# A chunked RWKV-7 scan on one core: state products taken by tokens, another order of the pass, the block solver shared between two engines

## The reference, cut to what matters

```python
def _rwkv_step(S, inp):
    r, w, kk, kka, kt, v = inp
    sk = jnp.einsum('bhij,bhj->bhi', S, kk)
    S = S * w[:, :, None, :] - sk[..., None] * kka[:, :, None, :] + v[..., None] * kt[:, :, None, :]
    return S, jnp.einsum('bhij,bhj->bhi', S, r)
```

## Time and profile before

| | us |
|---|---|
| median of 3 runs (3841.2 to 3844.97) | 3842.14 |
| profiled execution | 3850.02 |
| its span | 3848.3 |
| TensorE busy in the span | 3417.3 (89%) |
| VectorE, ScalarE, GpSimd busy | 1747.0, 1178.4, 552.4 |

### The profile page before, as it was taken

One profiled execution on the slowest core, in us unless ns is written; L12 is line 12 of the kernel. 1 busy time (PEld: TensorE's weight loads), 2 busy tenths in 40 slices (PEclk: granted clock), 3 DMA queues, 4 the chain that ended last, 5 costly groups with the idle time before them and its releaser, 6 DMA issues.

```text
span 3848.3 us, 65362 instructions
## 1 busy us (share of the span) xinstructions
PE 3417.3 (89%) x28861; PEld 2311.7 (60%) x28861; DVE 1747.0 (45%) x2909; ACT 1178.4 (31%) x2057; POOL 552.4 (14%) x754
## 2 busy tenths in 40 slices
PE   6999989999999898745776899898989999989998
PEld 5777776343343766545664443236757888756887
DVE  4324641121222654963356222126855546855454
ACT  3225722111111565921112111003253234334233
POOL 2220120000000210048513000001102210101210
PEclk8999998999999998867888899999999999989999
DMA  6531147989886352987533999993203313212322
GB/s 246 184 107 52 61 167 266 375 313 370 317 313 262 124 182 98 313 223 183 145 102 133 344 415 420 419 420 133 88 22 118 113 62 107 70 54 99 101 86 77
DMA packets 314859, 739.32 MB, mean 192 GB/s; under 512 B 68248, under 2 KB 148896, under 8 KB 265424
## 3 DMA queue, kind: packets, MB, share of 16 engines
q1 hardware_dynamic: 302480, 697.18, 49.7%
q0 software_dynamic: 12096, 37.96, 3.1%
HBM read 673.19 MB, written 61.89 MB: 191 GB/s over the span
## 4 chain that ended last, share of the span: by engine, by line
PE 70%; DVE 10%; DMA 8%; ACT 5%; issue 2%; SPq 2%; POOL 0%; DVEq 0%; POOLq 0%; ACTq 0%
PE ps L62 66%; DMA raw<-in_moe_w_dram 6%; PE ps L66 4%; SPq L120 2%; DVE mx L75 1%; DVE mx L102 1%; DVE mrn L99 1%; DVE b L75 1%; DVE cr L75 1%; DMA Tb<-ot 1%; DVE o L75 1%; DVE o L81 0%; ACT cr L72 0%; DMA c<-in_w_ple_gate_dram 0%; ACT lw L72 0%
## 5 line engine op out<-in xcount | busy, mean ns | idle before, releaser
L62 PE MATMUL ps<-raw,xinT 128*64 128x512 f32 (+1 forms) x4096 | 591.6, 492 | 32.8 <-DMA raw<-in_moe_w_dram 23.6
L62 PEld LDWEIGHTS ps<-raw,xinT 128*64 128x64 f32 (+1 forms) x4096 | 196.0, 123 | 401.4 <-issue 288.1
L62 PE MATMUL ps<-wp,hp 128*128 128x512 f32 x1024 | 314.1, 393 | 8.6 <-ACT wp L72 8.6
L62 PE MATMUL ps<-cr,oTr 128*128 128x512 f32 (+2 forms) x1024 | 255.6, 382 | 3.5 <-ACT oTr L72 3.1
L75 DVE TENSOR_TENSOR mx<-mx,ps 128x512 f32<-128x512 f32 (+1 forms) x196 | 127.3, 663 | 234.6 <-PE ps L62 133.3
L62 PEld LDWEIGHTS ps<-wp,hp 128*128 128x128 f32 x1024 | 193.8, 190 | 49.0 <-issue 8.8
L62 PEld LDWEIGHTS ps<-cr,oTr 128*128 128x128 f32 x1024 | 187.6, 188 | 38.9 <-ACT oTr L72 3.6
L62 PE MATMUL ps<-wp,hTr 128*128 128x512 f32 x512 | 194.4, 389 | 0.0
L62 PE MATMUL ps<-raw,hidT 128*64 128x512 f32 x768 | 177.9, 602 | 3.2 <-DMA raw<-in_moe_w_dram 3.2
L62 PE MATMUL ps<-ar,naxh 128*128 128x512 f32 x576 | 147.4, 406 | 19.0 <-DVE ar L75 8.8
L75 DVE TENSOR_TENSOR wp<-c,wp 128x1536 fp32r<-128x1536 f32 x32 | 60.6, 1894 | 180.7 <-ACT wp L72 180.7
(11 more groups left out here) (535 smaller groups left out, 6332.4 us busy)
## 6 DMA issues: line engine op xcount, KB each, us to landing
raw<-in_moe_w_dram SPq DMA_DIRECT2D x384, 1024.0 KB, 7.7
c<-in_w_in_dram SPq DMA_DIRECT2D x28, 2048.0 KB, 9.3
mx<-in_ada_w_dram SPq DMA_DIRECT2D x14, 2048.0 KB, 8.0
raw<-in_ada_w_dram SPq DMA_DIRECT2D x8, 2048.0 KB, 13.5
a<-in_na_w_qkv_dram SPq DMA_DIRECT2D x6, 2048.0 KB, 7.9
c<-in_w_branch_dram SPq DMA_DIRECT2D x16, 512.0 KB, 5.9
c<-in_w_out_dram SPq DMA_DIRECT2D x4, 2048.0 KB, 10.8
c<-in_w_ple_gate_dram SPq DMA_DIRECT2D x4, 2048.0 KB, 7.9
```

Of the source, the lines that this page charges most:

```text
L62: return self.e.matmul(out, lhsT, rhs, start=start, stop=stop, skip_group_check=True) if self.e is not None else self
```

## The change

- A by features, R, B and K are laid out as [R0, A0, A1, R1] and [B0, K0, K1, B1] (0 and 1 the halves of 64 tokens), so that a Gram product takes 128 columns of B and K against 128 of A and R: half as many products of twice the size. R and B are loaded in halves of 64 tokens.
- X and Y are one product: for a latent pass the output has 128 partitions, half of them X's tokens and half Y's. `y1` and `y2` go. What `y3` did comes as `y`, added into X's banks, and is done one half later, alternating with the products of `u` (`products_u`, `products_y`); X's banks are held until then. Y now lies by tokens, is copied by ScalarE (added by VectorE from step 4 on), and the readout needs no turn through TensorE.
- `v` and `s` are one product over 128 rows: V and U lie in one tile `VU` (two buffers), V loaded per pass and half, and the token rows of B and K in the matching halves. One bank instead of two; VectorE's sum is one operation, its decay two.
- Transfers: `load` 8 or 12, `load_m` 12, `load_t` 4. V for the readout (4 chunks) is loaded at pass 2.
- The solver: VectorE does chunk 0, rows 1 to 10 of chunk 1, and rows 24 to 31 of every later chunk as well, these at the head of an odd pass; GpSimd the rows between. The triangles of chunks 1 and 2 are loaded right behind chunk 0's. `store(n)` is in the list, at the head of the odd pass before it is used.
- `emm`: two additions instead of 22. Some tiles move into others that are free. `Banks.take` gives the free bank that was last used or released longest ago.

The diff, cut to its core (signs as in the diff; a few plain lines keep their place):

```diff
@@ class Banks @@
-        b = self.next % 8
-        self.next += 1
+        b = next(x for x in self.queue if x not in self.held.values())
+        self.last(b)
...
     def release(self, key):
-        del self.held[key]
+        self.last(self.held.pop(key))
@@ def rw_scan_order @@
     const()
-    load(0)
-    load_m(0)
-    load(1)
-    load_m(1)
+    for r in range(2):
+        load(r)
+        load_m(r)
+    rows(0, 1, 31)
+    store(0)
+    load_t(0)
     for s in range(4):
         gram(0, s)
     recur(0, 0, 'x1')
-    some(1)
-    load_t(0)
+    for n in range(1, 6):
+        rows(n, 1, LATE - 1)
     blocks(0)
     level(0, 0)
     level(0, 1)
     for r in range(12):
-        more = r + 1 < 12
+        more, n = r + 1 < 12, (r + 1) // 2
+        whole = more and r % 2
+        if more and not whole:
+            load_t(r + 1)
+        if more and r:
+            load_m(r + 1)
         if r + 2 < 12:
             load(r + 2)
-        if more:
+        if whole:
+            rows(n, LATE, 31)
+            store(n)
             load_t(r + 1)
-        some(3 if r else 8)
         recur(r, 0, 'x2')
-        recur(r, 0, 'y1')
-        recur(r, 0, 'y2')
-        one(r)
-        recur(r, 0, 'u')
-        recur(r, 0, 'v')
         if more:
             gram(r + 1, 0)
-            gram(r + 1, 1)
...
+        recur(r, 0, 'u')
+        one(r)
+        recur(r, 1, 'x1')
         recur(r, 0, 's')
         one(r)
+        if more:
+            gram(r + 1, 1)
+        one(r)
+        recur(r, 1, 'x2')
         if more:
             gram(r + 1, 2)
+            blocks(r + 1)
+        one(r)
+        recur(r, 1, 'u')
+        if more:
             gram(r + 1, 3)
+        recur(r, 1, 's')
         one(r)
...
         if more:
             level(r + 1, 0)
+            recur(r + 1, 0, 'x1')
             level(r + 1, 1)
         if r in (2, 9):
             rows_in(r)
+    recur(12, 0, 'u')
@@ def rw_scan, TensorE @@
+                for c in range(2):
+                    cols = pair(c) if lat(r) else keys(c)
+                    for p in range(2):
+                        k = 2 * g + i
+                        ins = e.matmul(P.psum[:, banks[p], i * 256 + cols.start:i * 256 + cols.stop], bk(r, z)[half(p), k, pair(c)], ar(r, z)[half(p), k, cols],
+                                       (i, c) == (0, 0), True)
...
+        def products_u(r, i, h):
+            b = P.banks.place.get(('u', r, i), 0)
+            for z in range(2):
+                o = half(1 - cut(z, i))
+                yield e.matmul(P.psum[o, b, sh(h)], Z(r, z)[o, h, :], X[o, sh(h)], h == 0, True)
+
+        def products_y(r, i, k, turn):
+            for z in range(2):
+                c, p = cut(z, i), z ^ turn
+                h = 2 * k + p
+                yield e.matmul(P.psum[half(c), P.banks.place.get(('x', r, i, p), 0), bank_of(z, k)], G(r, z)[half(1 - c), h, reads(c)],
+                               VU(r, z)[half(1 - c), i, sh(h)], False, True)
...
+                            out = P.psum[:, banks[p], bank_of(z, k)] if lat(r) else P.psum[half(1 - c), banks[p], bank_of(z, k)]
+                            ins = e.matmul(out, G(r, z)[half(c), h, pair(c) if lat(r) else keys(c)], VU(r, z)[half(c), i, sh(h)],
+                                           k == 0 and (turn == 0 or not lat(r)), False)
...
+                            ins = e.matmul(P.psum[half(p), b, bank_of(z, k)], tm(r, z)[:, c, sh(h)], VU(r, z)[:, i, sh(h)], (z, k) == (0, 0), True)
@@ def rw_scan, VectorE @@
+        def solve(n, i):
+            if n == 0 or i >= LATE or (n == 1 and i <= FIRST):
+                if n and i == LATE:
+                    e.wait_ge(*P.pool.at('row', n, i - 1))
+                solve_row(e, P.dve, n, i)
...
+            if what == 'u':
+                q, j = late(r, i)
+                if q >= 0 and step(q) >= 4:
+                    e.wait_ge(*P.pe.at('y', q, j))
+                    for z in range(2):
+                        for yo, src in parts(q, j, z):
                             e.tensor_tensor(yo, yo, src, ADD).then_inc(*P.dve.inc())
@@ def rw_scan, SyncE @@
+            squares(e, 0)
             fence(P, e, 'rw_features', *stored)
+            for n in (1, 2):
+                squares(e, n)
...
+        def store(n):
+            e.wait_ge(*P.dve.at('row', n, 31))
             for z in range(2):
+                e.dma_start(Td[z][ORDER[z][n]].rearrange("h (d n) -> (h d) n", d=4), Tv_of(n)[64 * z:64 * z + 64]).then_inc(*s_td[n].inc())
+            s_td[n].name('td', n)
+            if 1 <= n < 4:
+                squares(e, n + 2)
...
+                e.dma_start(ar(r, z)[:, :, 64:192], src['a']).then_inc(*s_ar[r % 3].inc())
+                e.dma_start(bk(r, z)[:, :, 64:192], src['k']).then_inc(*s_bk[r % 2].inc())
+                for c in range(2):
+                    if lat(r):
+                        e.dma_start(ar(r, z)[:, :, reads(c)], src['r'][:, :, half(c)]).then_inc(*s_ar[r % 3].inc())
+                    e.dma_start(bk(r, z)[:, :, reads(c)], src['b'][:, :, half(c)]).then_inc(*s_bk[r % 2].inc())
...
-                e.wait_ge(*P.pe.at('s', r - 2, 1))
+                e.wait_ge(*P.pe.at('recur', r - 2))
             for z in range(2):
...
+                for c in range(2):
+                    t = slice(chunk(r, z) * 128 + 64 * c, chunk(r, z) * 128 + 64 * c + 64)
+                    e.dma_start(VU(r, z)[half(c), cut(z, c), :], vd[t, f]).then_inc(*s_vu[r % 2].inc())
+                    e.dma_start(tm(r, z)[half(c), c, :], Tm['b', z][t, f]).then_inc(*s_tm[r % 2].inc())
+                    e.dma_start(tm(r, z)[half(1 - c), c, :], Tm['k', z][t, f]).then_inc(*s_tm[r % 2].inc())
```

More of the change, by code:

```diff
@@ L2757, in rows, with rw_scan_order @@
         self.s_g.name('readout')
-def rw_scan_order(const, load, load_m, load_t, gram, blocks, level, recur, solve, read, rows_in):
-    rows = iter(range(187))
+def rw_scan_order(const, load, load_m, load_t, gram, blocks, level, recur, solve, store, read, rows_in):
     reads = iter(READ)
-    def some(k):
-        for u in itertools.islice(rows, k):
-            solve(u)
     def one(r):
@@ L2773, in one, with rows @@
                 read(*x)
-    some(31)
+    def rows(n, first, last):
+        for i in range(first, last + 1):
+            solve(n, i)
     const()
-    load(0)
-    load_m(0)
-    load(1)
-    load_m(1)
+    for r in range(2):
[4 more added lines that the diff above has]
+    load_t(0)
     for s in range(4):
@@ L2971, in recur @@
                 for p in range(2):
-                    b, free = P.banks.take(('x', r, i, p), (P.act, 'x', r, i), hold=True)
+                    b, free = P.banks.take(('x', r, i, p), (P.dve if step(r) >= 4 else P.act, 'y' if lat(r) else 'x', r, i), hold=True)
                     banks.append(b)
@@ L3026, in recur @@
+                if q >= 0:
+                    for p in range(2):
+                        P.banks.release(('x', q, j, p))
+                    if j:
+                        P.pe.name('recur', q)
+            if what == 's' and not last:
+                e.wait_ge(*s_tm[r % 2].at('tm', r))
+                b, free = P.banks.take(('s', r, i), (P.dve, 'sum', r, i))
                 for f in free:
                     e.wait_ge(*f)
-                for h in range(8):
-                    for z in range(2):
-                        c = half(cut(z, i))
-                        ins = e.matmul(P.psum[c, b, sh(h)], Z(r, z)[c, h, :], XU[c, 0, sh(h)], h == 0, True)
@@ L3032, in recur @@
-                ins.then_inc(*P.pe.inc('u', r, i))
-            if what == 'v' and not last:
-                e.wait_ge(*s_tm[r % 2].at('tm', r))
-                banks = []
-                for z in range(2):
-                    b, free = P.banks.take(('s', r, i, z), (P.dve, 'sum', r, i, z), hold=True)
-                    banks.append(b)
-                    for f in free:
-                        e.wait_ge(*f)
-                for k in range(4):
-                    for z in range(2):
-                        for p in range(2):
-                            c, h = half(cut(z, i)), 2 * k + p
-                            ins = e.matmul(P.psum[half(p), banks[z], sh(k)], tm(r, z)[c, 0, sh(h)], V[c, chunk(r, z), hd(r, h)], k == 0, False)
-                ins.then_inc(*P.pe.inc())
@@ L3278, in load_t @@
         def load_t(r):
-            for z in range(2):
-                e.wait_ge(*s_td[z].at('td', step(r)))
+            e.wait_ge(*s_td[step(r)].at('td', step(r)))
             if r:
```

377 lines of the change are left out of this document (154 added, 223 removed).

## The result

The changed kernel takes 3946.51 us in the median (3946.09 to 3953.47, four runs), against 3843.55 for the kernel before on the same chip: 1.0273 times as long, with a 95% interval of 1.0255 to 1.0290. It is slower, as forecast, but by 103 us and not by 16; the range (up to 3882) does not hold it.

What follows compares the result with a forecast made beforehand. The scan was taken as a chain with no engine full. Start +2, leg 0 -1.1, legs 1 to 9 +19.3, leg 10 -4.0 and the rest 0 gave +16 us, 3866 profiled, so 3858 us in the median; range 3815 to 3882.

Steps and rivals of the forecast that it cites:

- the issue term of SyncE's chain: Odd legs of the scan: SyncE issues 24 token and feature transfers before the store, 12.3 us, taken as 13.5.
- the rule of banks: All stages: taking the oldest free bank adds no nameable TensorE wait elsewhere; 0, and -3 to +3 us if mergers reorder.
- TensorE's products: Latent scan passes: 768 matmul instructions fall to 512, some 2.6 us a leg by array time; typical even leg 21.2 us.
- The odd legs: Scan: late y, SyncE's loads, store, T's block load, VectorE and TensorE follow in a chain, 37.2 us a leg.
- Nothing hides it: Odd legs: no TensorE or VectorE work can cover the chain of 37.2 us, since all stands behind it in their queues.
- idle prices: Rival, odd legs: SyncE's chain holds but transfers land as in an empty queue, 30.5 us a leg, 3825 us; chance 0.24.
- TensorE alone bounds: Rival, scan: T is ready when wanted, so odd legs equal even ones at 21 us each, 3778 us; chance 0.08.
- 256-byte packets: Scan loads of R and B in halves: a 256-byte packet costs near 19 ns, making the loads 9.0 us of transfer.
- The rival of 32 ns: Rival, scan loads: 256-byte packets cost 32 ns, odd latent legs grow by 3.3 us, 3879 us; chance 0.16.
- r = 11 and the turns 0: Scan's end: one more y and its copy, +3 us, against two turns through TensorE lost, -3; together 0.
- Issue falls to 2 to 3 us a leg: Sign, scan: TensorE's waits for its own instructions, 4.1 us a leg before, fall to 2 to 3 us.
- Start "+2": Ahead of the scan's first product: solver rows moved to VectorE and 40 SyncE transfers before the first store, 2 us later.

Runs made afterwards that it cites:

- e3: The changed kernel with the store and the load of T's blocks ahead of the 24 token and feature loads in odd passes: 3893.29 us, ratio 1.0106.
- e9: The changed kernel with load(r+2) ahead of load_m(r+1), waiting for its buffer's last reader instead of the late Y: 3909.69 us, ratio 1.0166.
- e6: The changed kernel with x1 and x2 on 64x64 tiles and T's stores, block loads and later squares issued by GpSimd: 3873.54 us, ratio 1.0062.
- e7: As e6, but with the old rule of banks (next free one in a round) from the second network on: 3849.53 us, ratio 1.0000.
- e4: The changed kernel with each latent product x1 and x2 as two on 64x64 tiles, the same sums: 3920.69 us, ratio 1.0181.

## Why the prediction was right in sign and wrong in size

Three terms of the sum failed: the price of `x1` and `x2` on wide tiles, the issue term of SyncE's chain, and the rule of banks, which stood at nothing. The alternation of the legs and the chain of the odd ones were as forecast, though TensorE's wait in leg 5 was 16.9 us for 10 to 14 and the store started 22.3 us after S(5) for 17 to 19.

**TensorE's products: mis-sized, the main failure for the even legs.** "`x2` 1.1", "`x1`, `s` until 6.9", "`x1` 17.4". I priced `x1` and `x2` by count. They take 2.0 and 2.3 us at the full clock and 3.7 and 4.0 at the lower. For two of each in a latent leg this is about 4 us more than forecast at the full clock: 21.2 becomes 25.2, measured 25.7 in leg 4. With 64x64 tiles the legs were 21.6 and 21.8. In legs 8 and 10 more of the pass lay at the lower clock (0.66 and 0.60). "The Gram products halve in number but double in size, so their array time stays" was right (1.1 us a quarter for 1.0).

Leg 10 (35.0 us for 27) failed in one more way. The run with 64x64 tiles still has 31.3 us. TensorE stands 4.3 us there for ScalarE's copy of X, and ScalarE had waited 6.5 us for VectorE's part of the readout: not VectorE alone bounds this leg.

**The odd legs: the mechanism right, three terms too small.** Leg 5 by its own terms: until late `y` 5.0 (forecast 4.4); 24 issues 17.4 (13.5); from the store's issue to the blocks' 4.2 (5.3); block load 5.2 (5.5); VectorE 3.7 (4.0); `level`, `x1`, `level` 6.0 (4.5). The sum is 41.4 against 37.2. In leg 7 the same terms are 7.3, 16.2, 5.8, 4.4, 3.4 and 6.0: the late `y` itself comes later, behind an `x2` at the lower clock. The issue term failed because I took the 0.43 us of a transfer of 128 token rows for one of 64, which takes 0.60 (twelve of them: 2 us), and 1.2 us for stalls in the queue, which came to some 3; the last term failed because of `x1`. The store reached first (e3) and the earlier start (e9) both confirm the chain. What the forecast did not have is that `load_m`'s wait for the late `y` also closes a loop, through the feature rows and the first Gram product; in e6 and e7 this loop took what had been saved elsewhere.

**Legs 0 to 3,** 10.6 us over, are not explained one by one. Leg 2, 4.6 over, lay at a clock of 0.65; with the old rule of banks it was 20.4 us at 0.75.

**The rivals.** "Nothing hides it" was right: no odd leg came near the 30.5 us of "idle prices" or the 21 of "TensorE alone bounds".

**256-byte packets: right.** From 1860 to 1865 us there were 2153 packets under 512 bytes and 1578 longer ones, in 88 us of engine time (110% of 16 x 5 us; some cross the edges):

```profile
DMA packets 3732, 1.35 MB, mean 270 GB/s; under 512 B 2153, under 2 KB 3731, under 8 KB 3731
...
q1 hardware_dynamic: 3731, 1.33, 110.0%
```

With 32 ns for the longer ones the short ones cost 17 ns, where I took 19. Over five passes (1815 to 2000 us) the trace has 20480 packets of 256 bytes at 21 ns in the mean and 10240 of 512 bytes at 30. The rival of 32 ns falls. The rule of the Trainium skill ("DMA: Bandwidth & Descriptors", Specifications) would, as I had read it, have made 256 bytes as dear as 512; for these reads of DRAM the trace does not agree.

**The rule of banks: "0, and -3 to +3 us" was wrong,** with +23 us behind M, -5 to -10 in the scan and -6 to -8 ahead of it. I had looked for a wait that I could name in the profile of before. That view cannot show one: the waits came in a stage where the order in which banks come free is not the order in which they were taken. The sum needed each stage that holds banks or evicts out of order, gone through by hand.

**"r = 11 and the turns 0": wrong,** +10.2 us from S(11) to M (96.3 before, 106.5 after). r = 11 has the same dear products: its two `x2` take 3.68 us each, where they took 0.69. They are about half of it: in the five kernels with 64x64 tiles the stretch is 101.7 to 102.0 us. The other 5 us stay open.

**"Issue falls to 2 to 3 us a leg": more than right,** 1.4 us in the whole stretch. It came back in part with the count of instructions: with `x1` and `x2` on 64x64 tiles again it is 7.8 us (e4) to 24.1 (e6), where 41.1 stood before.

**Start "+2": wrong,** -6.6. From the start of chunk 0 on VectorE to S(0) the scan's head did get longer, by 5 us (43.1 for 38.1). The stage ahead gave 12: some 7 by the rule of banks, which I had at nothing, and some 5 by the granted clock of the first network in these two executions, which is luck.

In sum: forecast +16, measured +96 in the profiled pair, +103 by the medians. Start 9 less; legs 0 to 10 +69 where +14 was forecast, that is 55 more; r11 and readout 10 more; the second network 23 more. 9 less from 88 more is 79 to 80.

## What to carry over

Before you trade two small matmuls for one on a wider tile, price the instruction by the columns of its weights, not by the count: with 64 moving columns, an instruction with 128 columns of weights took three times as long as one with 64. With 128 moving columns it took 2.2 times as long, and the trade was even. When a transfer waits for "the pass is done", ask for the last reader of that very buffer, and follow what stands behind it in the queue: here such a wait closed a loop through SyncE that ate much of what was saved elsewhere. A change of an allocator is a change of every stage that uses it, so measure it alone first. And before you read a few microseconds off two single profiles, compare their granted clock in the stretches that no edit touches.

## What the runs showed of the hardware

- Matmul instructions of 64 rows by 128 columns of weights come at 62 ns each at the full clock (2.00 us for 32) and 115 at the lower, over 64 moving columns as over 32. On 64x64 tiles they come at 18 to 22 ns (1.16 us for 64, 0.69 for 32).
- A load of 64 rows of 2 KB is issued in 0.60 us, one of 128 rows in 0.43.
- 64 rows by 128 columns of weights over 128 moving columns come at 69 ns (1.11 us for 16), on 64x64 tiles at 31 ns (1.95 us for 62), both at the full clock.
- Between 480 and 740 us the granted clock was 0.97 in seven profiled executions and 0.94 or 0.95 in six, and with the same rule of banks the latter came 4 to 7 us later to the same instruction at about 1300 us.
